# A three-block kernel on one Trainium2 core: the third block's attention steps in another order, and its value loads issued by GpSimd

## What is computed

```python
h = einsum('btd,de->bte', x, w_in) + b_in            # 36 column tiles of 128
q_a, k_a, v_a, g_a, q_h, z_fwd, z_bwd, i_h, g_h = split(h)
o_a = neighbourhood_attention(q_a, k_a, v_a, rpb) * silu(g_a)   # 8 heads of 64
f = lb + (1 - lb) * sigmoid(z);  logf, k = log(f), 1 - f        # per direction
o_h = scan(q_h, k_fwd, i_h, logf_fwd) + flipped scan(q_h, k_bwd, i_h, logf_bwd)
o_h = rmsnorm(o_h) * gain * silu(g_h)                # 4 heads of 128
y = concat(o_a, o_h) @ w_out + b_out
return layernorm(2 ** 0.25 * x + y)
```

## Time and profile before

| what | us |
|---|---|
| runs (three) | 4486.35, 4489.6, 4497.59 |
| median | 4489.6 |
| profiled execution | 4494.11, with a span of 4492.2 |
| block 3, first projection to the end of the span | 1624.5 |
| PE busy in the span | 4224.4 (94%) |

### The profile page before, as it was taken

How to read it: one execution, slowest core, us unless ns; L and a number is a source line. 1 busy time by engine, 2 the same in 40 slices (tenths; PEclk the granted TensorE clock), 3 DMA queues, 4 the chain that set the end, 5 groups by cost and what they waited for, 6 DMA issues and landing times.

```text
span 4492.2 us, 62185 instructions
## 1 busy us (share of the span) xinstructions
PE 4224.4 (94%) x24346; PEld 3431.7 (76%) x24346; DVE 2695.9 (60%) x4235; ACT 1797.5 (40%) x3435; POOL 650.4 (14%) x305
## 2 busy tenths in 40 slices
PE   6999999999899989999899989988999999899689
PEld 5888888889788877788677768767888778777467
DVE  6788888871666533044367667556454564376666
ACT  5111111111566631122466656455354453266453
POOL 2111111110333311011011212322000000000112
PEclk9999999999999999999999999999999999999799
DMA  5111111122544421111479882577665655654653
GB/s 182 43 52 52 52 52 52 52 73 90 190 131 127 128 106 43 67 58 63 176 244 291 277 276 109 183 225 257 235 211 175 200 187 187 199 187 154 216 181 131
DMA packets 515500, 663.95 MB, mean 148 GB/s; under 512 B 60477, under 2 KB 407425, under 8 KB 491787
## 3 DMA queue, kind: packets, MB, share of 16 engines
q1 hardware_dynamic: 466778, 577.13, 39.7%
q10 hardware_dynamic: 48432, 82.85, 5.0%
HBM read 442.24 MB, written 217.65 MB: 147 GB/s over the span
## 4 chain that ended last, share of the span: by engine, by line
PE 79%; DVE 7%; DMA 5%; ACT 3%; SPq 3%; issue 2%; POOL 1%; ACTq 0%; DVEq 0%
PE ps L227 11%; PE ps L226 11%; PE ps L228 10%; PE ps L3749 4%; PE ps L3750 4%; PE ps L3751 4%; PE ps L252 3%; PE ps L251 3%; PE ps L253 3%; PE ps L3869 2%; PE ps L2214 1%; PE ps L239 1%; PE ps L3759 1%; PE ps L3761 1%; PE ps L3760 1%
## 5 line engine op out<-in xcount | busy, mean ns | idle before, releaser
L226 PE MATMUL ps<-hh,wsplit 128*128 128x512 f32 x2048 | 818.6, 400 | 9.7 <-DVE hl L1396 5.3
L227 PE MATMUL ps<-hl,wsplit 128*128 128x512 f32 x2048 | 814.6, 398 | 0.0
L228 PE MATMUL ps<-hh,wsplit 128*128 128x512 f32 x2048 | 808.9, 395 | 0.0
L963 DVE SCALAR_TENSOR_TENSOR conv_acc<-conv_in,pcol,conv_acc 128x1024 f32<-128x1024 f32 x480 | 687.9, 1433 | 14.8
L226 PEld LDWEIGHTS ps<-hh,wsplit 128*128 128x128 f32 x2048 | 387.2, 189 | 110.7 <-issue 8.1
L227 PEld LDWEIGHTS ps<-hl,wsplit 128*128 128x128 f32 x2048 | 390.0, 190 | 93.5 <-issue 4.3
L228 PEld LDWEIGHTS ps<-hh,wsplit 128*128 128x128 f32 x2048 | 385.9, 188 | 88.1
L3749 PE MATMUL ps<-h_hi,w 128*128 128x512 f32 x896 | 380.3, 424 | 17.9 <-ACT b_ost L3301 7.9
L218 POOL TENSOR_TENSOR wsplit<-wraw,wsplit 128x1024 fp32r<-128x1024 f32 x72 | 201.0, 2802 | 1338.7 <-ACT wsplit L213 1338.7
L3750 PE MATMUL ps<-h_lo,w 128*128 128x512 f32 x896 | 360.6, 402 | 0.0
L3751 PE MATMUL ps<-h_hi,w 128*128 128x512 f32 x896 | 359.0, 401 | 0.0
(11 more groups left out here) (405 smaller groups left out, 8797.7 us busy)
## 6 DMA issues: line engine op xcount, KB each, us to landing
w<-w_split_tiles SPq DMA_DIRECT2D x108, 1024.0 KB, 5.5
wraw<-in_w_in SPq DMA_DIRECT2D x72, 512.0 KB, 3.9
w_split_tiles<-w SPq DMA_DIRECT2D x36, 1024.0 KB, 6.7
sh<-hy_ak ACTq DMA_DIRECT2D x48, 512.0 KB, 3.7
g_tiles<-b_ost SPq DMA_DIRECT2D x80, 256.0 KB, 5.7
w_raw<-in_w_in SPq DMA_DIRECT2D x36, 512.0 KB, 4.5
wo_raw<-in_w_out SPq DMA_DIRECT2D x32, 512.0 KB, 6.1
sh<-hy_ad ACTq DMA_DIRECT2D x32, 512.0 KB, 9.2
```

What stands on the lines that cost most here:

```text
L226: e.matmul(p[:, :], wh, c.HH[tb][:, k, :], start=k == 0, stop=False)
L227: e.matmul(p[:, :], wh, c.HL[tb][:, k, :], start=False, stop=False)
L228: t = e.matmul(p[:, :], wl, c.HH[tb][:, k, :], start=False, stop=k == 7)
L963: e.scalar_tensor_tensor(v, a[:, h * 1024 + j:(h + 1) * 1024 + j], c.convw(j, ch), v, ALU.mult, ALU.add) \
```

## The change

1. **The order of a quarter's units** is given by strings. In quarters 0 to 2 the values of the first pairs of heads (`v0`) now come right behind the first head's keys, and `v1` behind the second head's, in place of the quarter's end; the quarters end with `ag3`. Quarter 3 begins with `ak0 aq0 v0` and ends with the four `rg`.
2. **Attention's steps** start at slot 34 and run one to a slot up to step 79 (slot 119), then two to a slot up to step 127 at slot 143. A visit starts when its keys, queries and values are projected, 4 or 5 slots on.
3. **The value loads** are issued by POOL (`values` in `b3_pool`), with the waits that they need of their own. They leave SP's list.
4. **Recurrence**: `el` always stands ahead of its slot's unit; its offsets are the same in all quarters but for the first head of quarters 1 and 2. The weights of the output projection, the chain and what follows stand one slot earlier.
5. Some semaphores are shared differently.

```diff
-        e = r + ((1, 2, 3, 4) if tb == 3 else (1, 2, 4, 5))[2 * d + h]
+        e = r + ((4, 5, 7, 8) if tb in (1, 2) and hd == 0 else (1, 2, 4, 5))[2 * d + h]
-        (after if tb == 3 else before)(e, "el", n)
+        before(e, "el", n)
...
+    heads = ["f0 rq0 rg0 aq0 ak0", "f1 rq1 rg1 aq1 ak1 ag1", "f2 rq2 rg2 aq2 ak2 ag2", "f3 rq3 rg3 aq3 ak3 ag3"]
+    orders = [
+        f"i0 i1 {heads[0]} v0 ag0 {heads[1]} v1 {heads[2]} {heads[3]}",
+        f"{heads[0]} i0 i1 v0 ag0 {heads[1]} v1 {heads[2]} {heads[3]}",
+        f"{heads[0]} i0 i1 v0 ag0 {heads[1]} v1 {heads[2]} {heads[3]}",
+        "ak0 aq0 v0 f0 i0 rq0 ag0 ak1 aq1 f1 rq1 ag1 v1 ak2 aq2 ak3 ag2 f2 rq2 aq3 i1 ag3 f3 rq3 rg0 rg1 rg2 rg3"]
...
+        first = max(free, ready[v] + (5 if tb < 3 else 4), 34 if v < 4 else 0)
+        for m in steps:
+            where[m] = first + (m - steps[0]) // (1 if v < 12 else 2)
+        free = where[steps[-1]] + 1
...
+    def values(v, g):
+        pr, groups, g0, g1 = L.visits[v]
+        s, cs = v % 2, slice(pr * 128, (pr + 1) * 128)
+        if g == g0:
+            if v >= 2:
+                e.wait_ge(*L.a_pe["val", L.last_step[v - 2]])
+            else:
+                e.wait_ge(*L.bd_st[v][v + 2, 1])
+        for t in (0, 2):
+            r = L.put_of[g // 2, "v", pr // 2, t]
+            e.wait_ge(*L.ost_st[r % 3][r])
+        for j in range(4):
+            src = c.VA[256 * g:256 * (g + 1), cs].rearrange("(r x) n -> r x n", x=64)[:, COL0[j]:COL0[j] + 32, :]
+            e.dma_start(L.V[:, s, 4 * (g - g0) + j, :], src).then_inc(*L.v_ld[s].up((v, g, j)))
```

More of the change, by code:

```diff
@@ L2692, in b3_layout @@
     L.ost_st = [dsig(f"b3_ost_st{i}", c.ost_out[i]) for i in range(3)]
-    L.f_a, L.f_d = sig("forget_by_act"), sig("forget_by_dve")
+    L.f_a, L.f_d = sig("forget_by_act", B1.stat), sig("forget_by_dve", B1.bn)
     L.r_pe, L.r_act, L.r_dve = sig("rec_pe"), sig("rec_act"), sig("rec_dve")
     L.qe_st, L.kv_st, L.o_st = [dsig(f"chain_q_st{i}") for i in range(4)], [dsig(f"chain_kv_st{i}") for i in range(2)], [dsig(f"rec_o_st{i}") for i in range(2)]
-    L.vis_ld, L.v_ld = [dsig(f"att_ld{i}", H.b_ld[i]) for i in range(2)], [dsig(f"att_v_ld{i}", H.k_ld[i]) for i in range(2)]
+    L.vis_ld, L.v_ld = [dsig(f"att_ld{i}", H.b_ld[i]) for i in range(2)], [dsig(f"att_v_ld{i}") for i in range(2)]
     L.sg_ld, L.y_st = [dsig(f"att_gate_ld{i}", H.b_ld[2 + i]) for i in range(2)], [dsig(f"att_y_st{i}", s) for i, s in enumerate((c.b2.pg_ld, c.b2.x_ld[1]))]
@@ L2729, in b3_order @@
     rq = {}
[L2731 to L2737, removed]
-    for tb in range(4):
[L2739 to L2772, removed]
@@ new lines, in b3_order, with unit @@
+    columns = {"f": 20, "rq": 16, "rg": 32, "aq": 0, "ak": 4, "ag": 12}
+    def unit(name):
+        kind, i = name[:-1], int(name[-1])
+        if kind in ("i", "v"):
+            pair(kind, i, {"i": 28, "v": 8}[kind] + 2 * i)
+        elif kind == "f":
+            for d in range(2):
+                col("f", (i, d), 20 + 4 * d + i)
+        else:
+            if kind == "rq":
+                rq[tb, i] = len(slots)
+            col(kind, i, columns[kind] + i)
+    heads = ["f0 rq0 rg0 aq0 ak0", "f1 rq1 rg1 aq1 ak1 ag1", "f2 rq2 rg2 aq2 ak2 ag2", "f3 rq3 rg3 aq3 ak3 ag3"]
@@ L2773, in b3_order @@
+    orders = [
[3 more added lines that the diff above has]
+        "ak0 aq0 v0 f0 i0 rq0 ag0 ak1 aq1 f1 rq1 ag1 v1 ak2 aq2 ak3 ag2 f2 rq2 aq3 i1 ag3 f3 rq3 rg0 rg1 rg2 rg3"]
+    for tb in range(4):
+        for name in orders[tb].split():
+            unit(name)
     assert len(slots) == 144 and len(L.tiles) == 144
+    at = {}
@@ L2776, in b3_order @@
+    for s, units in enumerate(slots):
+        at[units[0][2:5]] = s
     last = {}
@@ L2844, in b3_order @@
         after(12 + 6 * pr, "bias_st", pr)
[L2845 to L2854, removed]
-    for v, (pr, groups, g0, g1) in enumerate(L.visits):
-        ready = (36, 72, 108)[v // 4] if v < 12 else aq[pr] + 1
-        s = max(ready + 1, where[L.first_step[v]] - 6, where[L.last_step[v - 2]] + 2 if v >= 2 else 0)
+    where, free = {}, 34
+    ready = {}
+    for v, (pr, groups, g0, g1) in enumerate(L.visits):
+        tb = min(v // 4, 3)
+        ready[v] = max(at[tb, "ak", pr], at[tb, "aq", pr], at[tb, "v", pr // 2])
+        steps = range(L.first_step[v], L.last_step[v] + 1)
+        first = max(free, ready[v] + (5 if tb < 3 else 4), 34 if v < 4 else 0)
+        for m in steps:
+            where[m] = first + (m - steps[0]) // (1 if v < 12 else 2)
+        free = where[steps[-1]] + 1
+    assert free == 144
+    for v, (pr, groups, g0, g1) in enumerate(L.visits):
+        s = max(ready[v] + 1, where[L.first_step[v]] - 6, where[L.last_step[v - 2]] + 2 if v >= 2 else 0)
+        assert all(at[a // 2, "ag", pr] < where[L.first_step[v]] for a in groups)
         after(s, "visit", v)
@@ L2865, in b3_order @@
     for k in range(8):
-        after(149 if k < 4 else 151, "wo", k)
+        after(148 if k < 4 else 150, "wo", k)
     for k in range(0, 8, 4):
-        after(152 if k < 4 else 154, "wo_split", k)
-    c0 = 150
+        after(151 if k < 4 else 153, "wo_split", k)
+    c0 = 149
     for n in range(16):
@@ L3102, in visit @@
                 .then_inc(*L.vis_ld[s].up((v, h)))
[L3104 to L3111, removed]
     def bias_ld(pr):
@@ L3160, in b3_sp @@
             visit(s[1])
-        elif k == "values":
-            visit_values(*s[1:])
         elif k == "sg":
@@ L3722, in b3_pool @@
             w3_low(e, c, s[1])
+        elif k == "values":
+            values(*s[1:])
         elif k == "wo_split":
```

## The result

The changed kernel takes **4509.7 us** (median of 5, 4503.5 to 4515.1) against 4489.6 before: 1.0035 times as long, interval 1.0022 to 1.0048. The prediction was 4466, faster, with a range of 4447 to 4500; it was wrong in sign, and the time lies outside its range. The other 10 us of the difference between the medians no profile shows.

A forecast was written before the change was run, and what follows sets the result against it. PE was taken as the bound up to slot 143, hand-overs and loads after it. The terms -27 + 22 + 3 + 15 - 37 = -24 gave 4470 us for the profiled execution and 4466 for the median, range 4447 to 4500.

The forecast's parts named there:

- the slow clock behind the old waits: PE running slow behind long waits at four places: 4 us in all, counted in the gain from moving value loads.
- the slow clock behind three quarter ends: Slower clock after each longer quarter end: 0.9 us each, counted in the +15 for the three ends.
- Part 1: Value loads leave SP for POOL: PE's waits and slow stretches go, -27 us, with +3 for late loads.
- Part 2: Attention steps brought forward into the projection: PE reaches the end of slot 143 22 us later.
- Part 3: Three quarter ends lengthen, with a whole `el` ahead of the last `h_lo`: 5 us each, +15.
- Slots 0 to 34: Start of the projection: idle time stays, since its loads don't move; 0, give or take 5 us.
- Part 4: Last projection to first output matmul: 102 us instead of 139.3, so -37 (ends -51 and -15).
- Ahead of block 3, and behind the first output matmul: Behind the first output matmul nothing changes: 202 us stay.
- the third piece: Chain's first load to the output projection: 67 us instead of 75.8, with 64 as floor for 21 MB.
- POOL is slow: Rival: from 1.6 us an issue PE waits at four two-a-slot visits; at 2.15, +11 in all; chance 0.13.

The follow-up runs named there:

- e3_early_keys: Changed kernel, with key, query and bias loads one slot earlier and not waiting for `val`: 4481.0 us, 0.9988 of the kernel before.
- e1_order_alone: Changed kernel with its new order, but the value loads back in SP's list: 4484.4 us, 0.9986 of the kernel before.
- e4_quarter_ends: Changed kernel, with the turns of x tiles 2 and 3 put ahead of `el` at quarter ends: 4497.6 us, 1.0018 of the kernel before.

## Why the prediction was wrong, step by step

Terms in us, as predicted and as the profiled executions have them. Two of the prediction's own figures are used on the measured side, since no run shows them alone: 4 us for the slow clock behind the old waits, and 2.7 for the slow clock behind three quarter ends.

| Term | predicted | measured |
|---|---|---|
| Part 1, value loads by GpSimd | -24 | about -2 |
| Part 2, attention moved ahead | +22 | +25 |
| Part 3, three quarter ends | +15 | +23 |
| Slots 0 to 34 | 0 | +1 |
| Other idle time up to slot 143 | not priced | +3 |
| Part 4, the end | -37 | -40 |
| Ahead of block 3, and behind the first output matmul | 0 | 0 |
| Sum | -24 | +10 |

- **Part 1 is the step that failed.** What it says of `val` came true: no waits, and GpSimd took 10.7 us for 16 issues, 0.67 each, where 1.1 was put. The failure is in the budget: "a visit of 16 loads may begin at the `val` of step 79 (slot 121) and is wanted at step 84 (slot 124): three slots". It was worked out for the values alone. The keys and queries of the same visit wait for the same `val` and are wanted by `qk` two slots sooner, after one slot; they were counted as a gain ("for `att_q`, 1.1, whose loads stood behind value loads"). Within a visit the values had in truth stood behind them, and SP's queue had kept the two apart. What is measured: 19.2 us of waits and 5.6 of PE's busy time at a lower clock (344.94 in quarter 3, 339.30 in e3_early_keys) against 22.8 and 4 of gain. The prediction cited from the Trainium skill (DMA: Bandwidth & Descriptors, section Issuing engines are not separate DMA queues) that all issuers share the same DMA engines, and used it only to ask whether the gain would be zero. It never asked which transfer would be slowed. The 6 us for the landing of the last value load were also too few: at the visit shown GpSimd's loads took 6.9 to 10.7, without harm to `val`.
- **The gain itself was put down to the wrong half.** e1_order_alone has no `att_v` wait either. The waits were those of two visits released together; the order cures that.
- **Part 2** was right: PE's busy time up to the last projection rose by 29.4 us (1205.2 to 1234.6); less 5.6 and 2.7 for slow stretches, and with the 4 that went with the old waits, it is 25. So it rests in part on the two estimates above.
- **Part 3** was right at slots 71 and 107: 5 us of idle time each, 4.1 predicted, by `el` ahead of `h_lo` as e4_quarter_ends shows. It was mis-sized at slot 35, where the idle time rose by 10.7 (4.7 to 15.4). The prediction priced all three ends by the one at slot 71 and didn't look at the row loads; why they are late at slot 35 no run here settles.
- **Slots 0 to 34** kept their idle time, 32.5 and 33.2 us. (The prediction's 37 us is that of slots 0 to 35, with the quarter end in it.)
- **Part 4**: last projection to last `out` 24.2 (26 predicted), last `out` to the chain's first load 9.3 (9), from there to the output projection 65.7 (67). The store of `rec_o` was issued 2.1 us after the last `out`. The 64 us put as a floor for the third piece aren't one: from 4250 to 4272 the changed kernel moved 393 GB/s, more than the 329 it was worked out with.
- **The rival "POOL is slow"** had the right sign for a wrong reason: it priced GpSimd's issue at over 1.6 us. GpSimd issued at 0.67 us each, beside a DVE busy for 54% of quarter 3, and the loss came all the same. In the range no case stood for a transfer of the same visit being slowed.

## What to carry to other kernels

When loads leave a shared queue, list every transfer that stood ahead of them in it and ask when each is wanted: the queue's order was a priority, and a second issuer abolishes it. Work out the budget of every buffer that one event releases, not only of the one that is late today. And before a wait for a load is blamed on its issuer, look at how many loads one event lets go: here the new order alone gained 5 us where a second issuer alone cost 8. Last, when a wait gets shorter, check that the transfer did: the waiting engine may only have come later.

## What the runs showed of the hardware

- Sixteen loads of 64 KB issued by GpSimd beside a visit's key and query loads put the landing of `att_q` from 6.8 us (values held back) to 11.5 in the median, 15.1 at worst.
- GpSimd's issues are even: 0.675 to 0.677 us each in a run of 16, where SP's of the same loads were 0.505 to 1.129 at the same place.
- The same value loads take more of the DMA engines' time by GpSimd. The queues of the whole execution (kind: packets, MB, share of 16 engines), first before, then after, then with the values held:

```profile
q1 hardware_dynamic: 466778, 577.13, 39.7%
```

```profile
q1 hardware_dynamic: 432986, 560.34, 38.9%
...
q0 software_dynamic: 20480, 17.19, 2.1%
```

```profile
q0 software_dynamic: 20480, 17.19, 1.8%
```

  By the difference of SP's queue the 17 MB are 33792 packets and 0.8% there (0.7 and 1.1 between other pairs of runs); in GpSimd's they are 20480 packets and 2.1%. With the values held it is 1.8%. How much of a packet's time is waiting for its turn, and why the rest costs twice as much, was not tried.
